# Moving the gathered dot products and value sums of an expert layer to earlier tiles

## The reference, cut to what matters

```python
q = (xc @ w_q).reshape(t, PEER_HEADS, 2, PEER_QDIM // 2)
sc = jnp.einsum('thpc,hpnc->thpn', q, sub_keys)
v_half, i_half = lax.top_k(sc, PEER_TOPK_HALF)
...
top_s, pos = lax.top_k(cand, PEER_TOPK)
expert = jnp.take_along_axis(cand_idx, pos, axis=-1)
g = jax.nn.softmax(top_s, axis=-1)
u = u_tab[expert]
act = jax.nn.gelu(jnp.einsum('thkd,td->thk', u, xc), approximate=False)
w = (g * act)
return jnp.einsum('thk,thkd->td', w, v_tab[expert])
```

## Time and profile before

| | |
|---|---|
| median of 3 runs | 1942.85 us (1938.29 to 1945.58) |
| profiled execution: its own time, its span | 1940.13 us, 1938.4 us |
| TensorE matmuls busy | 1887.6 us (97%) |
| VectorE busy | 1594.6 us (82%) |
| ScalarE busy | 970.4 us (50%) |
| moved by DMA | 546.57 MB, 282 GB/s over the span |
| granted TensorE clock | 0.997 of full |

### The profile page before, as it was taken

How to read it: one execution, slowest core, us unless ns; L and a number is a source line. 1 busy time by engine, 2 the same in 40 slices (tenths; PEclk the granted TensorE clock), 3 DMA queues, 4 the chain that set the end, 5 groups by cost and what they waited for, 6 DMA issues and landing times.

```text
span 1938.4 us, 33523 instructions
## 1 busy us (share of the span) xinstructions
PE 1887.6 (97%) x11716; PEld 1683.7 (87%) x11716; DVE 1594.6 (82%) x3038; ACT 970.4 (50%) x1898; POOL 413.2 (21%) x348
## 2 busy tenths in 40 slices
PE   8999999999999999999999999999999999999998
PEld 7888887878999999987788888899999998877776
DVE  6899886886898879688888977779978886888887
ACT  6557644565311545355565666541135444555555
POOL 0000000000233344332232100003335442322220
PEclk9999999999999999999999999999999999999999
DMA  6544334525599999999999853359999999999995
GB/s 259 224 177 179 136 99 144 177 78 179 204 408 409 398 364 392 399 315 334 333 354 341 295 184 114 103 182 360 408 398 384 363 403 342 336 325 329 339 327 184
DMA packets 140841, 546.57 MB, mean 282 GB/s; under 512 B 14620, under 2 KB 14748, under 8 KB 138048
## 3 DMA queue, kind: packets, MB, share of 16 engines
q1 hardware_dynamic: 93760, 376.33, 54.2%
q0 software_dynamic: 46976, 168.91, 22.7%
HBM read 543.02 MB, written 1.05 MB: 281 GB/s over the span
## 4 chain that ended last, share of the span: by engine, by line
PE 57%; DMA 14%; DVE 10%; ACT 3%; issue 3%; SPq 0%; ACTq 0%; DVEq 0%
PE bank L2654 24%; DMA wbuf<-in_peer_v 10%; PE bank L350 7%; PE bank L352 7%; PE bank L351 7%; DMA wbuf<-in_peer_u 5%; PE bank L2685 3%; PE bank L2686 3%; PE bank L2503 2%; DVE tile_lo L3082 2%; ACT tile_hi L2807 1%; DVE x_tok L2440 1%; DVE tile_lo L280 1%; PE bank L2611 1%; DVE w_parts L3086 1%
## 5 line engine op out<-in xcount | busy, mean ns | idle before, releaser
L2654 PE MATMUL bank<-h_dense,wbuf 128*128 128x160 f32 x4096 | 575.0, 300 | 7.0 <-DMA wbuf<-in_peer_u 6.7
L2654 PEld LDWEIGHTS bank<-h_dense,wbuf 128*128 128x128 f32 x4096 | 558.7, 190 | 12.0 <-issue 6.9
L2807 ACT ACTIVATE tile_hi<-wbuf 128x1024 fp32r<-128x1024 f32 x248 | 261.5, 1056 | 243.8 <-DMA wbuf<-in_peer_v 211.2
L3082 DVE TENSOR_TENSOR tile_lo<-wbuf,tile_hi 128x1024 fp32r<-128x1024 f32 x256 | 308.4, 1221 | 77.5 <-ACT tile_hi L2807 75.6
L2416 POOL DMA_INDIRECT e_gbuf<-in_peer_v,e_row_at x128 | 174.1, 1360 | 405.6 <-DVE x_tok L2440 370.8
L2685 PE MATMUL bank<-tile_hi,w_parts 128*128 128x512 f32 x512 | 203.9, 398 | 8.8 <-DVE tile_lo L3082 5.6
L2416 POOL DMA_INDIRECT e_gbuf<-in_peer_rows,e_row_at x128 | 157.7, 1232 | 250.9 <-DVE e_dots L2434 138.5
L2686 PE MATMUL bank<-tile_lo,w_parts 128*128 128x512 f32 x512 | 199.8, 390 | 0.0
L352 PE MATMUL bank<-tile_hi,w_parts 128*128 128x512 f32 x512 | 199.4, 389 | 0.0
L350 PE MATMUL bank<-tile_hi,w_parts 128*128 128x512 f32 x512 | 199.4, 389 | 0.0
L351 PE MATMUL bank<-tile_lo,w_parts 128*128 128x512 f32 x512 | 199.4, 389 | 0.0
(11 more groups left out here) (426 smaller groups left out, 3614.9 us busy)
## 6 DMA issues: line engine op xcount, KB each, us to landing
wbuf<-in_peer_u SPq DMA_DIRECT2D x128, 1024.0 KB, 9.9
wbuf<-in_peer_v SPq DMA_DIRECT2D x256, 512.0 KB, 6.3
wbuf<-in_w_in SPq DMA_DIRECT2D x16, 2048.0 KB, 7.3
wbuf<-in_peer_q SPq DMA_DIRECT2D x32, 512.0 KB, 4.1
wbuf<-in_hyb_in SPq DMA_DIRECT2D x16, 512.0 KB, 4.0
wbuf<-in_mla_uq SPq DMA_DIRECT2D x9, 512.0 KB, 3.7
wbuf<-in_mla_in SPq DMA_DIRECT2D x8, 528.0 KB, 4.7
wbuf<-in_w_v SPq DMA_DIRECT2D x2, 2048.0 KB, 7.2
```

What stands on the lines that cost most here:

```text
L2654: last = nc.tensor.matmul(bank[:, j // 2 % 2, j % 2 * S + EXTRA:j % 2 * S + DENSE], deep[:, slot, k * P:(k + 1) * P], h_dense[:, k, PLAIN] ...
L2807: nc.scalar.activation(tile_hi[:, slot, 0:D], ring[:, slot, 0:D], ACT.Copy).then_inc(hi_done, 1)
L3082: nc.vector.tensor_tensor(tile_lo[:, slot, 0:D], ring[:, slot, 0:D], tile_hi[:, slot, 0:D].bitcast(F32), ALU.subtract).then_inc(lo_done, 1)
```

## The change

The number of items taken by a given tile of the U stage follows another line, in both expert layers.

```diff
     def taken_at(tile):
 
-        return min(34 + (tile - 48) * (DOTS - 34) // (121 - 48), DOTS + max(0, tile - 121) // 2)
+        return min(34 + (tile - 48) * (DOTS - 34) // (113 - 48), DOTS + max(0, tile - 118))
```

## The result

| | before | after |
|---|---|---|
| median of the runs | 1936.5 us (14 runs) | 1945.9 us (14 runs) |
| ratio of the runs | | 1.0052, 95% interval 1.0037 to 1.0067 |
| span of the profiled execution | 1938.4 us | 1947.5 us |
| mean granted clock of that execution | 0.997 | 0.993 |

The changed kernel is slower by 10 us (0.52% of 1936.5, interval 7 to 13; the two medians lie 9.4 us apart). The prediction said 0.5 us slower, at 1943.3 us, with 1936 to 1954 as the range. The time of 1945.9 us is only 2.6 us above the predicted one, but that is partly luck: the prediction started from the median of three runs, 1942.85 us, and the median of 14 is 1936.5. The change itself was mis-sized by some 10 us.

The account below looks back on a forecast made before the run. It took TensorE's own pace and a DMA system 94% full in the U stage as the limits. Terms 2.4 + 1 + 3.1 - 6 = +0.5 us gave 1940.6, plus 2.7 to the median: 1943.3 us, range 1936 to 1954.

Parts of the forecast that it names:

- Group 13: U stage, one-hots just in time: one more item ahead of them costs 1.2 us a layer, 2.4 us in all.
- granted clock as before: Sign for the whole kernel: the granted clock was to stay unchanged.
- DMA in the U stage: Tile 53 to 113: denser gathers fill the window at 410 GB/s and end late; 1 us in all.
- expected 210: Sign: DMA rate drops near 210 GB/s in the pause from tile 113 to 118.
- From U to V: Step between stages: two value sums a pair delay first V parts, doubled gathers delay V loads; costs 3.1 us, between 0 and 8.
- the fourth rival: V waits more: sums on odd tiles cost 9 us, the transition 8; 1963 at worst, 1953 at half; chance 0.05 for over 0.5%.
- the one gather ahead of a V load: Second layer's step to V: a doubled gather in front of a V load costs 1.3 us.
- The V stage: Seven fewer value sums and 3.7 MB less a layer shorten TensorE's late waits: a gain of 6 us.
- the 16.7 us: TensorE's small late waits in both V stages, 5.6 and 11.1 us, taken as the upper bound of the gain.
- The likeliest case: Whole kernel: time within 0.5%, 1933.1 to 1952.6 us, own range 1937 to 1950; chance 0.79.
- gathers late in front of VectorE: Rival, U stage: gathers become the bound and one-hots of groups 14 to 19 come late; 1969 or 1962 us, chance 0.08.
- a lower ceiling: Rival, U stage: DMA tops out at 359 GB/s, 22 us more a layer, 1987 us; chance 0.01.

Follow-up runs that it names:

- both places mended: Two items held back from tile 80 to 103 and no value sums behind the last two pairs: changed kernel 1.0005, kernel before 0.9992 of the kernel before.
- after_early: Changed kernel with three value sums behind each of pairs 59 to 61 and none behind the last two: 1.0071 of the kernel before.
- after_held: Changed kernel with two items held back from tile 80 to 103: 1.0052 of the kernel before.
- slope_only: Kernel before with only the denser dot products, 96 items by tile 113 and 99 at the V stage: 1.0027 of the kernel before.
- tail_only: Kernel before until tile 119, then two items for each pair, 104 when the V stage begins: 1.0048 of the kernel before.

## Why the prediction was right in time and wrong in size

- **Group 13** was right in mechanism and size: 2.4 us foreseen, 1.15 and 1.23 us more of waiting in the profile. The five items that should become six did, and no later group waits.
- **The clock was missing.** The prediction said "granted clock as before". The longer waits brought it down: behind group 13's wait of 2.5 us in seven of twelve places, for 1.65 us each (17.15 against 15.50 from group 12 to 14; 1.35 in one), and behind some V waits of 1.9 us and more. Over the runs the mean granted clock is 0.9946 and 0.9949 in the changed kernel's two sets, and 0.9960 in the 24 runs of the kernel before that stood beside the second: 0.0011 to 0.0014 of 1940 us, 2 to 3 us. With both places mended it is 0.9963 beside 0.9964, so the loss goes with the waits. The size is rough: each run's clock is given to 0.001, the first set ran at another time than the 24, and in every profile, before and after, the clock also falls between 325 and 330 us, a part that no version touches, for 3.4 or 6.8 us.
- **DMA in the U stage** was foreseen at 1 us and cost none. The bytes ran up towards the ceiling, if not to it: 391 GB/s (400 foreseen) from group 0 to tile 113, and 409 in the pause, where I had expected 210. So in the pause (409 - 203) x 15.2 = 3.1 MB, six gathers, still landed of the eight that had been issued ahead. The buffers took that up, and nobody waited. The loads got the 203 GB/s that TensorE's pace asks for, since TensorE didn't wait. The Trainium skill (DMA: Bandwidth & Descriptors, Queues, rings and completion order) says that an engine takes turns between queue rows; half of 409, 205 GB/s as an estimate by that rule, agrees with this trace's 203, but the loads asked for no more, so no run here tests it. The Trainium skill (HBM Reference, Specifications) gives about 358 GB/s as a core's share and about 425 for a core that streams alone; the 409 GB/s of this trace speak for the second.
- **From U to V** is the step that was mis-sized: "Sum 1.2 + 0.6 + 1.3 = 3.1 us". The two profiles of the changed kernel show 1.17 and 1.06 us more (first and second layer, on average) up to the first value matmul. In the first tiles they lose 4.3 and 2.8 us, the five profiles with 99 items 1.3 and 1.3: 3.0 and 1.5 more. Together 6.7 us, of which one fall of the clock in two profiles is 0.8. In the first layer the wait at the first value matmul was right (0.9 foreseen, 0.90 measured). What was missed is the loss from tile 4 to 16, 2.9 and 3.1 us; the sum had put nothing there, only the fourth rival had. In the second layer the sums did fit in VectorE's gaps, but the one gather ahead of a V load, 1.3 us, was too little: it measured 1.06 us up to the first value matmul and 1.5 in the first tiles, 0.8 of it the clock's.
- **The V stage** was to give back 6 us. What the rest of it loses is 5.6 and 7.0 us on average in the five profiles with 99 items, and 4.4 and 4.6 in the eight with 102 or more: 3.6 us in both layers, among draws from 0.1 to 10.5. So about half came, if it came: the uncertainty of these means is about 2 us. Where the first tiles lose most the rest loses least (6.0 and 0.1 in after_early, 4.5 and 1.5 in after_held), so a part of it may only be waits that moved forward; first tiles and rest together lose 15.2 us in the two layers of the profiles with 99 items and 14.8 in those with 102 or more. And the 16.7 us that the prediction took as what could be won were partly one unlucky draw.

The sum by these: 2.4 for group 13, 2.5 for the clock, nothing for DMA in the U stage, 5.9 from U to V without the clock, less 3.6 in V: 7.2 us, at the lower end of the 10 (7 to 13) measured. What may lie between is not settled; the single profiles move by more than that. The likeliest case was within 0.5% (1933.1 to 1952.6 us). As a time it held; as a change, 0.52% is just outside, and the interval (0.37 to 0.67%) doesn't decide. Of the rivals that end slower, gathers late in front of VectorE and a lower ceiling did not occur; the nearest is the fourth, by its transition.

## What to carry to other kernels

A schedule written by hand has a few places where the next engine is just in time, and only what stands in front of those counts: seven dots spread over 60 tiles cost nothing that the profiles show except the one in front of group 13, and value sums cost where the next stage's first loads and parts are due. Leave both the engine and the DMA queues clear there. Follow such a wait to its end: in the second layer TensorE's led to VectorE, from there to ScalarE, and from there to a V tile that had not landed. And before a stage's losses in one profile are taken as what can be won, look at a second profile of the same kernel: here one stage's length moved by 6.6 us between two of them.

## What the runs showed of the hardware

A wait of TensorE can cost more than its length. In the six profiles with the 2.5 us wait at group 13, the granted clock fell to its lower level for 3.4 us (2.9 in one) right behind it in all six first layers and in one second layer, and the matmuls up to group 14 took 9.15 us instead of 7.49 (8.85 in that one of 2.9). Behind the six waits of 1.37 us at the same place, and where no wait was left, it never fell. In the V stage it fell behind waits of 1.92, 2.50, 2.86 and 3.92 us and not behind 1.91 and 2.11. Why the second layer is spared more often at group 13 is open.

Loads land later the more gathers are issued beside them, but not in a straight line. In the 15 us around the first value matmul of the first layer the 512 KB V tiles landed after 4.1 us (median) beside two gathers of 512 KB (slope_only), 5.0 beside three (before), 5.4 beside six (changed kernel), 6.8 beside six (tail_only) and 8.0 beside seven (after_early).
